# A mixture of experts whose weights arrive in 1 MB pieces instead of 2 MB, with the next gather moved between the two layers

## The reference, cut to what matters

```python
N_EXPERTS, TOP_K, D_FF, MOE_BLOCK = 32, 4, 1024, 128

def moe_ffn(h, router_w, router_b, w1, b1, w2, b2):
    logits = (xt @ router_w + router_b).astype(jnp.float32)   # xt: 256 x 1024
    top_v, top_e = lax.top_k(logits, TOP_K)
    gates = jax.nn.softmax(top_v, axis=-1)
    ...                                                       # tokens sorted by expert, in blocks
    def expert_block(args):
        xblk, e = args
        act = clamped_swiglu(xblk @ w1[e] + b1[e])            # w1[e]: 1024 x 2048, 8 MB
        return act @ w2[e] + b2[e]                            # w2[e]: 1024 x 1024, 4 MB
    ...                                                       # each row times its gate, summed by token
```

## Time and profile before

| | us |
|---|---|
| three runs | 2466.84, 2473.72, 12914.3 |
| median of them | 2473.72 |
| the profiled execution's own time | 2466.25 |
| its span, first to last instruction | 2464.4 |
| TensorE busy | 2350.2 (95% of the span) |
| VectorE, ScalarE busy | 1386.3, 1009.5 |
| moved by DMA | 673.67 MB, of which 192 transfers of 2 MB are expert weights |
| mean granted TensorE clock | 0.988 of full speed |

### The profile page before, as it was taken

One profiled execution on the slowest core, in us unless ns is written; L12 is line 12 of the kernel. 1 busy time (PEld: TensorE's weight loads), 2 busy tenths in 40 slices (PEclk: granted clock), 3 DMA queues, 4 the chain that ended last, 5 costly groups with the idle time before them and its releaser, 6 DMA issues.

```text
span 2464.4 us, 35490 instructions
## 1 busy us (share of the span) xinstructions
PE 2350.2 (95%) x13360; PEld 1625.4 (66%) x13361; DVE 1386.3 (56%) x2592; ACT 1009.5 (41%) x1858; POOL 74.2 (3%) x125
## 2 busy tenths in 40 slices
PE   6999999999999999999989999999999889998999
PEld 3778854444444444444458888888888777776888
DVE  4677732332222233222267769886786677776785
ACT  3756521111111111111155555655655566674653
POOL 0000000000000000000000000000000111001000
PEclk8999999999999999999999999999999999999999
DMA  8764779999999999999965555555555655442553
GB/s 315 252 240 154 263 329 425 426 426 426 426 426 427 427 426 427 426 427 426 426 232 188 170 190 188 188 184 176 191 192 181 179 135 151 147 144 87 184 184 124
DMA packets 277970, 673.67 MB, mean 273 GB/s; under 512 B 8484, under 2 KB 236111, under 8 KB 244960
## 3 DMA queue, kind: packets, MB, share of 16 engines
q1 hardware_dynamic: 274656, 663.60, 70.6%
q0 software_dynamic: 3200, 8.53, 2.0%
HBM read 670.45 MB, written 1.12 MB: 273 GB/s over the span
## 4 chain that ended last, share of the span: by engine, by line
PE 85%; DVE 6%; ACT 5%; issue 3%; DMA 1%; DVEq 0%; ACTq 0%; SPq 0%
PE PS L372 26%; PE PS L1469 18%; PE PS L373 13%; PE PS L1491 9%; PE PS L1456 5%; PE PS L380 5%; PE PS L1443 3%; PE PS L381 2%; DVE WS L322 1%; ACT WS L318 1%; DVE XG L1586 1%; PE PS L2072 1%; DMA RAW<-in_w_ada 1%; PE PS L765 1%; PE PS L2087 1%
## 5 line engine op out<-in xcount | busy, mean ns | idle before, releaser
L372 PE MATMUL PS<-HN,WS 128*128 128x512 f32 x1952 | 697.1, 401 | 14.9 <-DVE WS L322 9.2
L322 DVE TENSOR_TENSOR WS<-RAW,WS 128x1024 fp32r<-128x1024 f32 (+1 forms) x452 | 540.8, 1205 | 139.5 <-ACT WS L318 134.3
L373 PE MATMUL PS<-HN,WS 128*128 128x256 f32 x1952 | 548.2, 281 | 0.0
L318 ACT ACTIVATE WS<-RAW 128x1024 fp32r<-128x1024 f32 (+1 forms) x452 | 463.2, 1035 | 84.0 <-PE PS L373 69.8
L1469 PE MATMUL PS<-RING,XG 128*64 128x512 f32 x2048 | 446.5, 594 | 10.9 <-DVE XG L1586 10.9
L372 PEld LDWEIGHTS PS<-HN,WS 128*128 128x128 f32 x1952 | 368.2, 189 | 106.9 <-DVE WS L322 11.5
L373 PEld LDWEIGHTS PS<-HN,WS 128*128 128x128 f32 x1952 | 370.8, 190 | 0.3
L1469 PEld LDWEIGHTS PS<-RING,XG 128*64 128x64 f32 x2048 | 149.1, 137 | 294.1 <-issue 293.4
L1592 DVE TENSOR_SCALAR GLU<-PS 128x256 f32<-128x256 f32 x64 | 27.2, 425 | 413.2 <-PE PS L1469 413.2
L372 PE MATMUL PS<-MI,WS 128*128 128x512 f32 x704 | 245.4, 394 | 0.0
L1491 PE MATMUL PS<-RING,AT 128*64 128x512 f32 x1024 | 226.8, 594 | 14.8 <-ACT AT L1365 14.8
(11 more groups left out here) (356 smaller groups left out, 2539.0 us busy)
## 6 DMA issues: line engine op xcount, KB each, us to landing
RING<-in_moe_w SPq DMA_DIRECT2D x192, 2048.0 KB, 21.6
RAW<-in_ffn_w_in SPq DMA_DIRECT2D x88, 1024.0 KB, 5.1
RAW<-in_attn_w_qkv SPq DMA_DIRECT2D x36, 1024.0 KB, 5.0
RAW<-in_ffn_w_out SPq DMA_DIRECT2D x32, 1024.0 KB, 4.9
RAW<-in_w_ada SPq DMA_DIRECT2D x24, 1024.0 KB, 8.3
RAW<-in_w_in SPq DMA_DIRECT2D x22, 1024.0 KB, 5.7
RAW<-in_ffn_w_out SPq DMA_DIRECT2D x16, 768.0 KB, 4.2
RAW<-in_conv_w_in SPq DMA_DIRECT2D x12, 1024.0 KB, 5.1
```

Source lines behind the costliest of these rows:

```text
L318: act_f(split_tile(0, n), raw_tile(n), ACT.Copy).then_inc(hi_done, 1)
L322: vec.tensor_tensor(split_tile(1, n), raw_tile(n), split_tile(0, n).bitcast(f32), ALU.subtract).then_inc(lo_done, 1)
L372: nc.tensor.matmul(both, hi[:, k, :], x2[:, :, kx, :], start=start, stop=False)
L373: ins = nc.tensor.matmul(half, lo[:, k, :], x2[:, 0, kx, :], start=False, stop=stop)
```

## The change

Four things, all in the expert stage.

1. **Pieces of 1 MB, eighteen homes.** Each piece is cut into two, 8 KB in each partition; an expert has twelve. A ninth pair of homes is added at `ub0`, in memory for which 4 KB are newly set aside (`KD` and the `QRAW` tiles of the attention stages move there). Homes are numbered in another order, the loop is unrolled three experts at a time instead of four, and TensorE still waits for pieces by pairs (`wait_piece`), but counts each one when it is done with it. The first eighteen pieces, one and a half experts, are fetched ahead; the last two of these wait for `mask_ready`.
2. **The next gather between the layers.** `gather(d + 1)` stands behind the first layer of block d. For that, VectorE no longer takes the expert's column of ranks: `select` finds from the global ranks which token is in the next block, whichever expert that is, and the ranks count on over all blocks (a matmul from `ROW64` adds the blocks before).
3. **Turning ahead of the combine.** The transposes stand ahead of `combine`, in banks 0 and 1.
4. **The bias behind the first pair of pieces**, not ahead of the first layer.

The last expert has its own code (`last_one`): its combine of the block before is moved ahead of the first layer, and behind the second layer stand `combine(d + 1)` and one more gather, which nobody needs but which VectorE waits for.

```diff
-            w, q = (w1, i) if i < 4 else (w2, i - 4)
-            src = w[e, q] if isinstance(e, int) else w[ds(e, 1), q].rearrange("a p k n -> (a p) k n")
+            w, q, half = (w1, i // 2, i % 2) if i < 8 else (w2, (i - 8) // 2, i % 2)
+            src = w[e, q, :, half] if isinstance(e, int) else w[ds(e, 1), q, :, half].rearrange("a p n -> (a p) n")
             p = ring_place(g, i)[0]
-            sp.dma_start(RING[p][:, :].rearrange("p (k n) -> p k n", k=2), src).then_inc(piece_loaded[p], 16)
+            sp.dma_start(RING[p][:, :], src).then_inc(piece_loaded[p // 2], 16)
...
+            def gather(d):
+                pe.wait_ge(sem("p_ready"), d)
...
             def expert(...):
                 with pe.Fori(0, blocks.of(e)):
                     d = blocks.now()
-                    pe.wait_ge(sem("p_ready"), d)
-                    for k in range(DC):
...
-                    for j in range(2):
-                        nc.tensor.matmul(bank[j][:, :], EH[:, :], B1S[:, 512 * j:512 * (j + 1)], start=True, stop=False)
                     pe.wait_ge(sem("xg_ready"), d)
+                    pe.wait_ge(sem("pgt_ready"), d)
                     for q in range(4):
...
-                        last.then_inc(sem("mm1_done"), 1)
-                    combine(d)
-                    for tt in range(TT):
-                        last = nc.tensor.transpose(bank[6][:, tt * P:(tt + 1) * P], PGAT[:, tt, :], IDENT)
-                    last.then_inc(sem("pgt_mm"), 1)
+                            if j == 1:
+                                last.then_inc(sem("mm1_done"), 1)
+                            elif q == 3 and k == 1:
+                                last.then_inc(sem("mm1_half"), 1)
+                        if q == 0:
+                            pe.wait_ge(sem("e_taken"), e + 1)
+                            for j in range(2):
+                                nc.tensor.matmul(bank[j][:, :], EH[:, :], B1S[:, 512 * j:512 * (j + 1)], start=False, stop=False)
+                    if not last_one:
+                        gather(d + 1)
                     for j in range(2):
                         pe.wait_ge(sem("ac_ready"), d * 2 + (j - 1))
+                        if j == 1:
+                            pe.wait_ge(sem("pgat_ready"), d)
+                            for tt in range(TT):
+                                last = nc.tensor.transpose(TURNED_GATES[:, tt * P:(tt + 1) * P], PGAT[:, tt, :], IDENT)
+                            last.then_inc(sem("pgt_mm"), 1)
...
+                    if not last_one:
+                        combine(d)
...
+                    if last_one:
+                        combine(d + 1)
+                        gather(d + 1)
...
+            def select(d):
+                def step(ins, n):
+                    ins.then_inc(sem("picked"), 1)
+                    dve.wait_ge(sem("picked"), d * PICKED + (n - PICKED))
+                step(STT(SELV[:, :, :], RANK[:, :, :], SLOTS + 0.5, RANK[:, :, :], ALU.is_lt, ALU.mult), 1)
+                step(vec.tensor_reduce(RKE[:, :], SELV[:, :, :], AX.X, ALU.max), 2)
+                for tt in range(TT):
+                    last = TS(PSEL[:, tt, :], SLOT[:, 0:SLOTS], RKE[:, tt:tt + 1], None, ALU.is_equal)
+                last.then_inc(sem("p_ready"), 1)
...
                     times_sigmoid(1)
-                    add_sums(d)
-                    dve.wait_ge(sem("rk_next"), d)
+                    if last_one:
+                        add_sums(d + 1)
+                    dve.wait_ge(sem("xg_mm"), d + 1)
+                    take_gathered()
+                    if not last_one:
+                        add_sums(d)
                     dve.wait_ge(sem("pgt_mm"), d)
                     blocks.end()
...
             n0 = by_name["gate1_0"].n0
             lo_tile(dve, n0)
             dve.wait_ge(sem("ff_sq"), 3)
```

More of the change, by code:

```diff
@@ L53, in constants @@
     before = np.triu(np.ones((P, P), f), 1)
[L54 removed]
+    slot = np.tile(np.arange(1, SLOTS + 1, dtype=f), (P, 2))
     small = np.concatenate([ident, before, slot], axis=1)
@@ L1446, in pe @@
             pe.wait_ge(sem("b1_split"), 3)
-            def expert(fours, g):
-                e = fours * UNROLLED + g
-                pe.wait_ge(sem("e_taken"), e + 1)
+            def gather(d):
+                pe.wait_ge(sem("p_ready"), d)
+                for k in range(DC):
+                    for tt in range(TT):
+                        last = nc.tensor.matmul(GATHERED[:, k * SLOTS:(k + 1) * SLOTS], H2K[:, tt, k * P:(k + 1) * P],
+                                                PSEL[:, tt, :], start=tt == 0, stop=tt == TT - 1)
+                last.then_inc(sem("xg_mm"), 1)
@@ L1451, in expert @@
+            def expert(turn, g, last_one=False):
+                e = turn * UNROLLED + g
+                if last_one:
+                    pe.wait_ge(sem("e_taken"), NE)
+                    combine(blocks.now())
                 with pe.Fori(0, blocks.of(e)):
                     d = blocks.now()
-                    pe.wait_ge(sem("p_ready"), d)
-                    for k in range(DC):
-                        for tt in range(TT):
-                            last = nc.tensor.matmul(bank[4][:, k * SLOTS:(k + 1) * SLOTS], H2K[:, tt, k * P:(k + 1) * P],
-                                                    PSEL[:, tt, :], start=tt == 0, stop=tt == TT - 1)
@@ L1474, in expert @@
[L1474 to L1478 removed]
+                                                        w[k][:, 1024 * side + 512 * j:1024 * side + 512 * (j + 1)],
+                                                        start=q == 0 and k == 0, stop=q == 3 and k == 1)
@@ L1491, in expert @@
                                 last = nc.tensor.matmul(bank[6][64 * side:64 * side + 64, :], AT[:, b, 64 * q:64 * q + 64],
-                                                        w[:, b, 512 * side:512 * (side + 1)],
+                                                        w[:, D * (b % 2) + 512 * side:D * (b % 2) + 512 * (side + 1)],
                                                         start=q == 0 and b == 0, stop=q == 1 and b == 3)
-                        last.then_inc(sem("mm2_done"), 1)
+                            if b % 2 == 1:
+                                last.then_inc(sem("mm2_done"), 1)
+                    if last_one:
+                        combine(d + 1)
+                        gather(d + 1)
                     blocks.end()
-            with pe.Fori(0, NE // UNROLLED) as fours:
+            gather(1)
+            with pe.Fori(0, TURNS_E) as turn:
                 for g in range(UNROLLED):
-                    expert(fours, g)
-            d = blocks.now()
-            pe.wait_ge(sem("p_ready"), d)
-            combine(d)
-            for _ in range(9):
-                nc.tensor.matmul(bank[5][:, 2 * P:4 * P], MEAN[:, :], SM[:, 0:2 * P], start=True, stop=True)
+                    expert(turn, g)
+            for e in range(TURNS_E * UNROLLED, NE):
+                expert(TURNS_E, e % UNROLLED, last_one=e == NE - 1)
+            keep_warm(pe, 6, 0)
             for tt in range(TT):
```

175 lines of the change are left out of this document (106 added, 69 removed).

## The result

| | before | after |
|---|---|---|
| median of 12 runs each, same chip | 2467.84 us | 2478.8 us |
| ratio, without the run of each that lies far out | | 1.0039, 95% interval 1.0028 to 1.0051 |
| the profiled execution's own time, its span | 2466.25, 2464.4 | 2474.9, 2473.1 |
| from span start to the scaling behind the last expert | 1255.84 | 1265.40 |
| from there to the end | 1208.56 | 1207.7 |

The forecast was 2475.3 us and no change that 2% can tell. The kernel is slower by 0.4%: the profiled execution lies 0.4 us under the forecast, the median 3.5 us over it. One of the twelve runs on each side lies far out (12914.3 us before, 3968.9 us after, this one at a granted clock of 0.553 of full speed) and is in the medians but not in the ratio. Behind the scaling nothing differs by more than single runs do. So 9.56 us have to be found ahead of it.

The account below looks back on a forecast made before the run. TensorE was taken to set the time, with the weight stream right behind it. The earlier 2466.25 us plus 6.1 for the stream and 3.0 behind the last expert gave 2475.3 us; range 2461 to 2488.

Parts of the forecast that it names:

- What bounds: Expert stage: TensorE's 28.8 us an expert sets the time, the stream's 29.5 stands behind; TensorE's saved 29 us count nothing.
- Run size: First-layer weight stream: runs of 8 KB instead of 16 KB lower it from 428.9 to 421.5 GB/s, +10.4 us.
- Small packets of the added transfers: Weight stream: 182 added transfers each end with one small packet per engine, at 10.8 ns; +2 us (0 to 4).
- Restart: Stream's start in the first expert: the first 1 MB home comes free 1.75 us into the first layer, -1.75 us.
- The gap: First expert's stream: smaller pieces leave little queued before the second layer's first home is free; +0.5 us (0 to 1.5).
- Two more MB ahead: Weight stream: 18 MB instead of 16 lie ready at the start, so 2 MB less follow; -4.9 us.
- The start: First expert's first layer starts where it did, with select replacing the loop's entry; -0.15 us (-0.4 to +0.6).
- The tail: Behind the last expert: VectorE waits for the spare gather; scaling 8.3 us after the combine, +3.0 us (0 to 3.5).
- Run size a third or none: Second layer's lower rate comes from two regions per transfer; a third of packet terms gives 2467, chance 0.12; none 2463, 0.08.
- Something of its own in 1 MB transfers: Weight stream: 1 MB transfers move at 348 GB/s because of their size; time 2666 us, chance 0.05.
- Stream doesn't bind: Expert stage: TensorE's 27.9 us an expert count, the stage ends 25 us sooner; time 2445 us, chance 0.02.
- Spare gather hidden: Behind the last expert: the spare gather adds no visible time; time 2472 us, chance 0.08.

## Why the prediction was right, point by point

- **What bounds.** Right. TensorE has the shorter expert (27.9 forecast, 27.85 measured) and is priced at nothing. Waits were forecast from about expert 15, some 31 us in all: they begin in expert 15 at 764.98, and 16 experts grow by 1.97 us, 31.5 (TensorE's own row of waits shows 24.7 of it as idle time). The forecast's two lines, 30.0 e - 7.9 and 27.9 e + 24.3, give 32.9 at the last expert, not 31. The kernels with idle matmuls show the slack, 31.9, from the other side.
- **Run size.** The mechanism is right and the size near: +10.4 forecast, +8.9 by the kernel that changes nothing else. The Trainium skill (DMA: Bandwidth & Descriptors, section Why small descriptors are slow) with its 3 cycles would give a third of it; 16, 8 and 4 KB at 429, 421.5 and 407 say otherwise, and the measurement decides.
- **Small packets of the added transfers.** +2 forecast (0 to 4), +0.35 measured. Its reading, a fixed cost for the small packets too, is not borne out. The same page of the Trainium skill (section Bandwidth) has 341 GB/s for 1 MB, issued from GpSimd; queued by SyncE they ran at 422 here, so it is no figure for such a queue.
- **Restart.** SyncE's first issue comes 1.97 us behind the first layer, 1.72 sooner than before: -1.75 was right. The gap was forecast at +0.5 (0 to 1.5) and is 2.6: 1.9 in the second layer of expert 0, and 0.7 at 340 to 344 us, which the step did not have. It took a home that comes free before the queue is empty as enough. The home came free as forecast (issue at 357.24, 22.97 us behind the start; 22.6 forecast), and the dip came all the same. The step left out that a transfer issued brings its first bytes only later (the issue at 336.24 moved nothing until 337.0), and that the next homes follow no sooner than TensorE frees them (358.95, 360.67).
- **Two more MB ahead.** -4.9, not tried alone. Nine homes against eight, both with the old runs and the new order, differ by 6.1 us up to the last combine once the slower second layer is taken off (916.98, 923.11).
- **The start.** Forecast -0.15 (-0.4 to +0.6), measured +1.71, outside its bounds, as the gap is: these are the two steps that failed. About 0.55 was there already at 311 us (a row of the mixer at 311.43 against 310.88). The rest is the clock: the warm-up rows grow by 1.69, and some 0.6 of that is taken back because the gather no longer waits behind them. The step took the warm-up matmuls as the same, and they are, but had no term for a fall of the clock under them. Those in the routing ahead were thinned out, from three together to one and one (the profile counts each as two). Before, then after:
```profile
322.11 1.54 PE L1251 MATMUL PS<-SM,MEAN 128*128 128x256 f32 x6
```
```profile
322.44 0.68 PE L1272 MATMUL PS<-SM,MEAN 128*128 128x256 f32 x2
...
324.63 0.70 PE L1272 MATMUL PS<-SM,MEAN 128*128 128x256 f32 x2
```
With three in place of one at one of these places the clock stayed at 1.00; but it did so once without them, so this cause is likely and not shown.
- **The tail.** +3.0 forecast, +2.39 measured: 7.75 us where 8.3 stood. The 0.5 for leaving the loop is what was too much: L322 follows the 0.6 of `XG` at once. The open wait for `AC` in the last expert was not foreseen; it ends before the last pair lands, and so costs the changed kernel little.
- **The sum** of these terms by the runs: 1.71 - 1.72 + 2.6 - 4.9 + 8.9 + 0.35 = +6.9 up to the last pair, where 7.35 was measured (1.71 + 5.64). 0.4 us stay open, and the -4.9 is the forecast's own, since no run has it alone. The forecast had +6.1. That the total came within 0.4 us is luck: the start and the gap, too low by 1.86 and 2.1, and the open 0.4 stood against the run size, the small packets and the tail, too high by 1.5, 1.65 and 0.6, and 0.86 less behind the scaling.
- **The rivals.** Run size a third or none: out. Something of its own in 1 MB transfers: out. Stream doesn't bind: out. Spare gather hidden: it was not, VectorE waited 2.17 us for it; between the last expert's layers it is hidden in part (2.36 us less in the tail, 1.65 more in the last expert).

## What to carry to other kernels

When an engine and a stream stand within 2 or 3% of each other (28.8 and 29.5 us an expert here), cost both to the end: a shorter step of the engine is worth what the stream's slack leaves, and a kernel with idle work added at that step measures this slack directly. When cutting transfers in two to free homes sooner, look at what it does to each partition's contiguous run: here halving the run cost 8.9 us, the cut itself 0.35, and the finer homes gave back 1.7. Transfers of 1 MB with runs of 16 KB were not tried. Whoever moves a step ahead of the one that frees buffers should look at the first turn of the loop, where the queue is shortest. And a forecast that is right in its total may rest on errors that cancel: each term wants its own landmark.

## What the runs showed of the hardware

- A queued weight stream on one core: 429, 421.5 to 422 and 407 GB/s with runs of 16, 8 and 4 KB; one transfer of 2 MB or two of 1 MB make 0.35 us of difference in 905.
- TensorE's granted clock was 0.53 of full speed over 2 us of warm-up matmuls behind thinned routing, and back at 1.00 some 4 us later. Five of six kernels with that routing show such a fall, one does not. It fell again in the last expert of three kernels, where TensorE had just waited 1.37 and 0.46 us for `AC`: the second layer took 8.78, 8.78 and 8.63 us in place of 7.09.
```profile
1244.00:1248.00 4.00, 0.62 1.09 349
```
```profile
1272.00:1276.00 4.00, 0.60 0.00 0
```
```profile
1258.00:1262.00 4.00, 0.59 1.09 345
```
The first row is of the kernel with nine homes, the others of those with four and with three idle matmuls. In three more kernels, the changed one among them, the same wait was followed by full clock. What decides it, these runs do not show.
